# QK-norm of a streaming encoder layer: sums of squares as two-row products, inverse roots spread through memory

## The reference

```
z  = rms_norm(x) @ w_in
qa = rms_norm(qa.reshape(B, T, 8, 64), qn_a)      # FoX queries; the keys ka likewise
qb = rms_norm(qb.reshape(B, T, 4, 2, 64), qn_b)   # Diff queries; the keys kb likewise
rms_norm(x, g) = x * rsqrt(mean(x*x over the last 64) + eps) * g
```

## Time and profile before

| | |
|---|---|
| median of 3 runs | 2223.88 us (2221.85 to 2227.34) |
| profiled execution, span from first to last instruction | 2221.3 us |
| TensorE busy | 2098.9 us, 94% |
| VectorE busy | 963.1 us, 43% |
| ScalarE busy | 792.3 us, 36% |
| GpSimd busy | 109.1 us, 5% |
| mean granted TensorE clock | 0.950 |

### The profile page before, as it was taken

One profiled execution on the slowest core, in us unless ns is written; L12 is line 12 of the kernel. 1 busy time (PEld: TensorE's weight loads), 2 busy tenths in 40 slices (PEclk: granted clock), 3 DMA queues, 4 the chain that ended last, 5 costly groups with the idle time before them and its releaser, 6 DMA issues.

```text
span 2221.3 us, 33304 instructions
## 1 busy us (share of the span) xinstructions
PE 2098.9 (94%) x12679; PEld 1980.5 (89%) x12679; DVE 963.1 (43%) x1613; ACT 792.3 (36%) x1427; POOL 109.1 (5%) x182
## 2 busy tenths in 40 slices
PE   5999999999999999999869999999999999999997
PEld 4988898898988889898758999999999999999987
DVE  5433334324344353444436523755355435544542
ACT  3444444435344454545332223433122212212321
POOL 3100100101001000100000000000000000000001
PEclk8998999889999899989779999999999999999999
DMA  5220401303212130212124322011111111111112
GB/s 195 70 68 10 129 20 30 118 10 97 60 30 79 26 92 9 86 30 58 41 100 128 130 87 68 29 47 43 53 34 46 38 52 38 37 49 46 37 52 72
DMA packets 149045, 135.64 MB, mean 61 GB/s; under 512 B 5160, under 2 KB 131218, under 8 KB 148960
## 3 DMA queue, kind: packets, MB, share of 16 engines
q1 hardware_dynamic: 130368, 68.95, 11.0%
q0 software_dynamic: 18592, 65.46, 9.0%
HBM read 103.56 MB, written 30.83 MB: 61 GB/s over the span
## 4 chain that ended last, share of the span: by engine, by line
PE 84%; DVE 6%; issue 3%; ACT 3%; DMA 2%; POOL 0%; DVEq 0%; ACTq 0%; SPq 0%; POOLq 0%
PE bank L613 44%; PE psS L613 21%; PE psO L613 14%; PE psT L800 3%; DMA gate<-gate_scr 2%; DVE pT_l L1319 1%; ACT pT_h L958 1%; PE bank L673 1%; DVE m_a L1539 1%; PE psT L613 1%; DVE sc L1472 0%; DVE m_b L1539 0%; DVE w_l L1319 0%; PE bank L728 0%; PE psT L642 0%
## 5 line engine op out<-in xcount | busy, mean ns | idle before, releaser
L613 PE MATMUL bank<-xn_hi,w_h 128*128 128x364 f32 (+1 forms) x952 | 336.7, 354 | 22.0 <-DVE xn_lo L1319 11.7
L613 PE MATMUL bank<-xn_lo,w_h 128*128 128x364 f32 (+1 forms) x952 | 325.5, 342 | 0.0
L613 PE MATMUL bank<-xn_hi,w_l 128*128 128x364 f32 (+1 forms) x952 | 324.8, 341 | 0.0
L613 PEld LDWEIGHTS bank<-xn_hi,w_h 128*128 128x128 f32 x952 | 190.8, 200 | 33.3 <-issue 21.0
L958 ACT ACTIVATE w_h<-wraw 128x1024 fp32r<-128x1024 f32 x133 | 139.6, 1050 | 216.4 <-PE psO L613 206.5
L1134 ACT ACTIVATE sc<-sc,small 128x1024 f32<-128x1024 f32 (+5 forms) x144 | 118.7, 824 | 250.1 <-DVE small L1457 250.0
L613 PEld LDWEIGHTS bank<-xn_lo,w_h 128*128 128x128 f32 x952 | 190.7, 200 | 0.0
L613 PEld LDWEIGHTS bank<-xn_hi,w_l 128*128 128x128 f32 x952 | 189.5, 199 | 0.0
L1319 DVE TENSOR_TENSOR w_l<-wraw,w_h 128x1024 fp32r<-128x1024 f32 x133 | 162.2, 1220 | 39.0 <-ACT w_h L958 38.9
L1258 ACT ACTIVATE ct<-u,vecs 128x1090 f32<-128x1090 f32 x44 | 57.2, 1300 | 327.6 <-DVE u L1598 327.6
L613 PE MATMUL psS<-x_l,w_h 128*128 128x364 f32 (+1 forms) x528 | 173.7, 329 | 0.0
(11 more groups left out here) (310 smaller groups left out, 4600.1 us busy)
## 6 DMA issues: line engine op xcount, KB each, us to landing
wraw<-in_w_up SPq DMA_DIRECT2D x44, 512.0 KB, 3.9
wraw<-in_w_in SPq DMA_DIRECT2D x41, 512.0 KB, 4.0
gate<-gate_scr POOLq DMA_DIRECT2D x16, 544.0 KB, 4.4
wraw<-in_w_down SPq DMA_DIRECT2D x16, 384.0 KB, 3.2
wraw<-in_w_down SPq DMA_DIRECT2D x16, 320.0 KB, 2.9
x_scr<-xT POOLq DMA_DIRECT2D x8, 544.0 KB, 3.7
cum_s<-c_scr POOLq DMA_DIRECT2D x8, 544.0 KB, 7.9
gate_scr<-zv POOLq DMA_DIRECT2D x8, 544.0 KB, 5.0
```

The costliest lines, as they stand in the source:

```text
L613: return pe.matmul(out, w, x, start=first, stop=last, **kw)
```

## The change

The sums of squares become products with `half_ones` as the weights (two columns) and the squares as the moving operand, 364 columns at a time. Six jobs SQ0 to SQ2 and SK0 to SK2 take the place of SS0 and SS1; ScalarE copies each [2, 364] result to the first two rows of `sqq` or `sqk`. SP writes these rows to memory (`ms_scr`), reads them back as [128, 34] into `meansq`, and after Sqrt and reciprocal writes `root` out (`rt_scr`) and loads each of the four rows into the 64 partitions of its head. NQ and NK go; a unit has 32 jobs in place of 34. The plans are rearranged around this. In SP's queue the new steps stand between the loads of G0 and G1.

```diff
-        gaps = {-1: [["Q0"], ["Q1"]], 7: [["Q2"], ["SS0", "K0"]], 8: [["K1"], ["K2", "V0"]],
-                6: [["SS1"], ["V1"]], 5: [["V2"], ["NQ0", "VT0"]], 4: [["NQ1", "VT1"], ["VT2", "NQ2"]],
-                3: [["G00"], ["NK0", "NK1"]], 2: [["NK2", "KC0"], ["G01"]], 1: [["KT0", "KT1"], ["G02"]],
-                0: [["KT2", "KC1", "/G10"], ["G10"]]}
+        gaps = {-1: [["Q0"], ["Q1"]], 7: [["Q2"], ["SQ0", "SQ1", "K0"]], 8: [["SQ2", "K1"], ["K2", "V0"]],
+                6: [["SK0", "SK1"], ["SK2", "V1"]], 5: [["V2"], ["VT0"]], 4: [["VT1"], ["VT2"]],
+                3: [["G00"], ["KC0"]], 2: [["KC1"], ["G01"]], 1: [["KT0", "KT1"], ["G02"]],
+                0: [["KT2", "/G10"], ["G10"]]}
...
-        gaps = {-1: [["Q0"], ["Q1"]], 7: [[], ["Q2", "K0"]], 8: [["SS0", "KC0"], ["K1"]],
-                6: [["K2"], ["SS1", "V0"]], 5: [["V1"], ["V2"]], 4: [["VT0", "VT1"], ["VT2", "G00"]],
-                3: [["NQ0", "NQ1"], ["G01", "NQ2"]], 2: [["NK0"], ["G02"]], 1: [["NK1", "NK2"], ["G10"]],
-                0: [["KT0", "KT1"], ["KT2", "KC1"]]}
+        gaps = {-1: [["Q0"], ["Q1"]], 7: [[], ["Q2", "K0"]], 8: [["SQ0", "SQ1", "KC0"], ["SQ2", "K1"]],
+                6: [["K2"], ["SK0", "SK1", "V0"]], 5: [["SK2", "V1"], ["V2"]], 4: [["VT0"], ["VT1", "G00"]],
+                3: [["VT2"], ["G01"]], 2: [["KC1"], ["G02"]], 1: [["KT0"], ["G10"]], 0: [["KT1"], ["KT2"]]}
...
-PROLOGUE_PLAN = ["F0", "F1", "F2", ("W", "K"), "Q0", "Q1", "Q2", ("FORGET",), ("W", "V"), "K0", "K1", "K2",
-                 "KC0", "KC1", "SS0", "SS1", ("NORM",), "V0", "NQ0", "NQ1", "NQ2", "NK0", "NK1", "NK2", ("SCALE",),
-                 "V1", "KT0", "KT1", "KT2", ("SPLIT", 0, 1), "V2", "VT0", "VT1", "VT2", ("WFIRST",), ("SPLIT", 2)]
+PROLOGUE_PLAN = ["F0", "F1", "F2", ("W", "K"), "Q0", "Q1", "Q2", ("FORGET",), ("W", "V"), "K0", "SQ0",
+                 "K1", "SQ1", "K2", "SQ2", "SK0", "SK1", "SK2", "KC0", "KC1", "V0", "V1", ("NORM",), "V2", "VT0", "VT1",
+                 "VT2", ("SCALE",), "KT0", "KT1", "KT2", ("SPLIT", 0, 1), ("WFIRST",), ("SPLIT", 2)]
...
+    if nxt:                                   # Sqrt and reciprocal move from behind SS1 to behind V2
+        then["V2"] = then["V2"] + [("ROOT",)]
+        later["V2"] = later["V2"] + [("RD",)]
+        later[SCALE_AFTER[kind]] = later.get(SCALE_AFTER[kind], []) + [("SCALE",)]
+SCALE_AFTER = {"A": "KC1", "B": "G01"}
...
+        def spread_roots(count, n):
+            sp.wait_ge(S["pj_d"], count)
+            sp.dma_start(ms_scr[0:2], sqq[0:2, :]).then_inc(S["ms_o"], 16)
+            sp.dma_start(ms_scr[2:4], sqk[0:2, :]).then_inc(S["ms_o"], 16)
+            sp.wait_ge(S["ms_o"], n * 32 + 32)
+            sp.dma_start(meansq[:], ms_scr.rearrange("r t -> (r t)").rearrange("(p c) -> p c", p=P)
+                         ).then_inc(S["ms_i"], 16)
+            sp.wait_ge(S["rt_d"], n + 1)
+            sp.dma_start(rt_scr.rearrange("r t -> (r t)").rearrange("(p c) -> p c", p=P), root[:]
+                         ).then_inc(S["rt_o"], 16)
+            sp.wait_ge(S["rt_o"], n * 16 + 16)
+            for x, dst in enumerate((sqq, sqk)):
+                for h in range(2):
+                    sp.dma_start(dst[DH * h:DH * h + DH, :], rt_scr[2 * x + h:2 * x + h + 1].broadcast_to([DH, T])
+                                 ).then_inc(S["rt_i"], 16)
+        spread_roots(J1["SK2"], 0)            # prologue, before the loads of unit 0
...
-            for g in range(2):
-                load_w(wraw[:], U.block(f"G{g}"), gv[U.u][g])
+            load_w(wraw[:], U.block("G0"), gv[U.u][0])
+            if U.nxt:
+                spread_roots(U.j0 + U.job["SK2"], U.u + 1)
+            load_w(wraw[:], U.block("G1"), gv[U.u][1])
...
+            elif kind in ("SQ", "SK"):
+                pe.wait_ge(S["pj_d"], base_of(f"{kind[1]}{c}"))
+                c0, m = CHUNKS[c]
+                sq = sqq if kind == "SQ" else sqk
+                r = mm(bank[0:2, 0:m], half_ones[:, 0:P:DH], sq[:, c0:c0 + m], True, True)
...
-            act.wait_ge(S["pj_d"], J1["SS1"] if U is None else U.j0 + U.job["SS1"])
+            act.wait_ge(S["ms_i"], 16 if U is None else U.u * 16 + 32)
             act.activation(root[:], meansq[:], ACT.Sqrt, bias=eps_t).then_inc(S["sq_rt"], 1)
...
+            dve.wait_ge(S["rt_i"], 64 if U is None else U.u * 64 + 128)
+            for z, q, g in ((zq, sqq, gq_a if kind == "A" else gq_b), (zk, sqk, gk_a if kind == "A" else gk_b)):
                 r = dve.scalar_tensor_tensor(z[:], z[:], g, q[:], ALU.mult, ALU.mult)
```

More of the change, by code:

```diff
@@ L87, in unit_plan @@
     end = ["SPLIT", "G11", "G12", "OT0", "OT1", "OT2"] if nxt else ["OT0", "OT1", "OT2"]
-    then = {"SS1": [("ROOT",)], **({"G02": [("H", "FIRST")]} if nxt else {}),
+    then = {**({"G02": [("H", "FIRST")]} if nxt else {}),
             **{a: [("H", b)] for a, b in WEIGHTS_AFTER[nxt].items()}}
-    later = {"SS1": [("RD",)], "NK2": [("SCALE",)], **({"G02": [("L", "FIRST")]} if nxt else {}),
+    later = {**({"G02": [("L", "FIRST")]} if nxt else {}),
              **{a: [("L", b)] for a, b in WEIGHTS_AFTER[nxt].items()}}
+    if nxt:
+        then["V2"] = then["V2"] + [("ROOT",)]
+        later["V2"] = later["V2"] + [("RD",)]
+        later[SCALE_AFTER[kind]] = later.get(SCALE_AFTER[kind], []) + [("SCALE",)]
     pending = []
@@ L189, in build @@
     c_scr = nc.dram_tensor("c_scr", (2, H_A, T), F32).ap()
+    ms_scr = nc.dram_tensor("ms_scr", (4, T), F32).ap()
+    rt_scr = nc.dram_tensor("rt_scr", (4, T), F32).ap()
     def alloc(stack):
@@ L212, in build @@
     rsub = small[:, 26:35]
-    meansq = sb("meansq", [P, NT, 2, 2])
-    root = sb("root", [P, NT, 2, 2])
+    meansq = sb("meansq", [P, 4 * T // P])
+    root = sb("root", [P, 4 * T // P])
     inv0 = sb("inv0", [P, NT])
@@ L693, in job @@
                     return
[L694 to L697 removed]
+            elif kind in ("SQ", "SK"):
+                pe.wait_ge(S["pj_d"], base_of(f"{kind[1]}{c}"))
+                if U is None and name == "SQ0":
                     pe.wait_ge(S["cst"], 5)
[L699 to L711 removed]
+                c0, m = CHUNKS[c]
+                sq = sqq if kind == "SQ" else sqk
+                r = mm(bank[0:2, 0:m], half_ones[:, 0:P:DH], sq[:, c0:c0 + m], True, True)
             elif kind == "VT":
@@ L1024, in evacuate @@
                 r = copy(zv[:, tok], src)
-            elif kind == "SS":
-                r = copy(meansq[:, 0:8, c, :], bank[:, 0:16].rearrange("p (t h) -> p t h", h=2))
-                r = copy(meansq[0:T_S, 8, c, :], bank[0:T_S, 16:18])
-            elif kind in ("NQ", "NK"):
-                t0, m = TGROUPS[c][0] * P, (3 * P if c < 2 else 2 * P + T_S)
-                r = copy((sqq if kind == "NQ" else sqk)[:, t0:t0 + m], bank[:, 0:m])
+            elif kind in ("SQ", "SK"):
+                c0, m = CHUNKS[c]
+                r = copy((sqq if kind == "SQ" else sqk)[0:2, c0:c0 + m], bank[0:2, 0:m])
             elif kind in ("VT", "KT"):
@@ L1375, in normalize @@
             kind = "A" if U is None else U.next_kind
-            for name, z, q, g in (("NQ2", zq, sqq, gq_a if kind == "A" else gq_b),
-                                  ("NK2", zk, sqk, gk_a if kind == "A" else gk_b)):
-                dve.wait_ge(S["pj_d"], J1[name] if U is None else U.j0 + U.job[name])
+            dve.wait_ge(S["rt_i"], 64 if U is None else U.u * 64 + 128)
+            for z, q, g in ((zq, sqq, gq_a if kind == "A" else gq_b), (zk, sqk, gk_a if kind == "A" else gk_b)):
                 r = dve.scalar_tensor_tensor(z[:], z[:], g, q[:], ALU.mult, ALU.mult)
```

22 lines of the change are left out of this document (1 added, 21 removed).

## The result

| | before | after |
|---|---|---|
| median | 2224.41 us (4 runs, 2221.85 to 2227.34) | 2275.95 us (4 runs, 2263.74 to 2286.26) |
| ratio after to before | | 1.023, 95% interval 1.0195 to 1.0265 |
| span of the profiled execution | 2221.3 us | 2262.2 us |
| mean granted clock | 0.950 | 0.941 |

The profiled execution is the quickest of the four after; the others had mean clocks of 0.937, 0.933 and 0.928 and took 2273.6, 2278.4 and 2286.3 us.

What follows compares the result with a forecast made beforehand. TensorE, busy 94% of the span, was taken to bound the kernel. Work and waits +28.3 and clock -2.4 gave +26 on the profiled 2221.3 us, plus 2.6 to the median: 2250 us, range 2217 to 2277.

Steps and rivals of the forecast that it cites:

- Dearer: Rival: two-row products do not hold the clock and every stall brings a long dip; +15, 2265 us; chance 0.20.
- Work and waits, clock aside: Whole kernel without clock effects: prologue +5.0, four A units -2.4, three B units +25.7, together +28.3 us.
- K1: Prologue: with SQ0 between, K1 waits for K0's evacuation by ScalarE; 4.5 us later, 3.9 idle.
- A's K0: A units, tile 7, second map: K0 waits for SQ0's evacuation behind the exp; 2.4 us later, 3.1 idle.
- KC0: B units, tile 8, first map: KC0 waits for SQ0's copy behind the exp; +2.6 us, 3.3 idle.
- ScalarE before G1's copy: B units: G1's load queues behind roots and spread on SP; ScalarE stalls 5.9 us, +7.2 us a unit (bounds +4 to +10).
- KT0: Prologue: TensorE idles 7.3 us before KT0, waiting for roots, spread and scaling.
- B's tile 4: B units: the root's 1.6 us on ScalarE delays tile 4's product, which already waits 0.72 us for VectorE.
- The trip: Roots through memory in B units: small write 2.3 us, spreading loads of 1.1 MB about 6.4 us.
- Net -2: Clock over the whole kernel: 44 us returned by the sums, 42 lost to new stalls; bounds -24 to +16.
- six stalls: B units: two new stalls in each, priced at 3.5 us of clock apiece, 21 us together.
- the root at tile 5: A units: the moved root delays the copy of the next transposes on ScalarE; next product waits, +0.8 us.

Runs made afterwards that it cites:

- g3: Changed kernel with each two-row product of the sums issued twice, the second overwriting the first with the same values: 2283.06 us, ratio 1.0288.
- e1: Changed kernel with the square-sum jobs spread over the slots, so no long job stands two places behind a short one of its slot: 2246.19 us, ratio 1.0106.
- e2: Changed kernel with G1's load issued before the roots are written out and spread: 2250.21 us, ratio 1.0131.
- f4: Kernel before the change with each square-sum job cut from nine two-column products to one of 18 columns (norm computed wrongly): 2166.73 us, ratio 0.975.
- e0: The repeat: changed kernel as it is, run again as base for the other runs: 2273.58 us, ratio 1.0222.
- f2: Changed kernel with the root and its table loads behind the copy of transposed probabilities of A's tile 5 (second map) and B's tile 4: 2268.2 us, ratio 1.0197.
- f3: Changed kernel with the edits of e1, e2 and f2, B's scaling moved, and the prologue's K1 and root reordered: 2200.82 us, ratio 0.9895.
- g1: f3 with the root and table loads ahead of G0's first chunk on ScalarE, and A's last V transposes in their old place: 2191.22 us, ratio 0.986.
- e3: Changed kernel with the Sqrt of units 0 to 6 replaced by a copy, so no table loads (norm computed wrongly): 2238.19 us, ratio 1.0078.
- f1: Changed kernel with three more products, never read, ahead of the transposes of each V block: 2263.0 us, ratio 1.015.
- g2: f3 with the Sqrt of units 0 to 6 replaced by a copy, so no table loads (norm computed wrongly): 2177.63 us, ratio 0.9797.
- h1: g1 with A's jobs reordered so each conversion ahead of a copy of transposed probabilities has a long product beside it: 2175.96 us, ratio 0.979.

## Why the prediction was right, and which term was off

Forecast 2250, measured 2276: slower, as said, but by 51.5 us and not by 26. The time lies 1 us inside the upper end of the range (2277), so that the range held by little; the rival "Dearer" (2265) came nearer in number, though g3 shows that half of its mechanism is false.

**Work and waits, clock aside: right in sum, and in part by luck.** Up to unit 7's first scores the trace is 46.7 us longer. TensorE idles 66.5 us more than before (125.6 against 59.1), and 41.6 us of work are gone: +24.9, where the sum had +28.3. By stage, idle time added against what the sum implied (its term plus the 5.2 us a norm that left, with the 1.0 us wait before unit 0's Q0 counted in A): prologue 15.7 against 11.2, A 13.1 against 17.4, B 37.7 against 41.3. In A 7.0 us of this are the two waits at the loop's turn that went, of which the prediction used one as a price for the clock and expected neither to go. Without them A's waits are 20.1 and the sum +32. So the new waits were put some 4 us too low, and an unforeseen gain of 7 hid it.

**Step by step.** K1 3.54 us of idle (3.9 said), A's K0 2.93 (3.1), KC0 3.33 (3.3), ScalarE before G1's copy 4.96 (5.9), KT0 8.91 (7.3). The first scores came at 135.5 (131.3): V's transposes end 1.6 us later than said, the wait behind them is 1.6 longer, and from KT0 to the scores it takes 6.5 us and not 5.5, at half clock. The mechanisms are also shown by removal: e1 takes the bank waits away and 27 us, e2 the queue order and 23. In B's tile 4 the delay of the root was put at 1.6 us on ScalarE; the wait went from 0.72 to 2.67.

**Durations.** Two-row products: 0.32 us said, 0.31 to 0.35 from start to start. The trip was quicker in the write of the roots (1.5 to 1.8 us against 2.3) and slower in the spread (in unit 5 first issue 920.9, last landing 928.4, 7.5 us against 6.4; up to 8.1 in the others); these nearly cancel. The Trainium skill (DMA: Bandwidth & Descriptors, section "Anatomy of one DMA - SWDGE (gpsimd) path") gives 2.0 us fixed plus bytes over 436 GB/s. The trace differs on both sides: 1.5 to 1.8 us for 17 KB, 7.5 for the 1.1 MB that it puts at 4.6; these DMAs leave SP's queue, though, not GpSimd's.

**The clock: the term that was off.** It is "Net -2": 44 us given back by the sums, 42 lost to new stalls. TensorE's busy time up to unit 6 fell by 19.9 us (1000.2 to 980.3) where 41.6 of work left: the clock took 22, not -2. By stage: prologue 0, A +6, B +16. The first half of the step had the mechanism right and the size a little high: by f4 the two-column sums cost 32 or 33 us of clock, not 44, and by g3 two-row products cost none, against the rival "Dearer". The second half was too low in two places.

In B, six stalls were priced at 21 us, and more places than these lose the clock. The half clock of the first trace after (81.9 us, against 34.2 before) stands in four places: 27.4 us at KC0's bank wait (units 5 and 6), 13.6 behind the root at tile 4, 30.6 at the wait for G1's weights, 10.2 behind a wait of 1.4 us for VectorE's scores, which has no term. e1 has none of it at KC0, e2 6.8 at G1; other stretches grow in their place, so that the totals fall by less.

In A, the step priced K0's stall (2.0; the trace has 3.4 to 6.8 us of half clock behind it in three units, none in unit 3) and gave the root at tile 5 0.8 us of waiting and no clock. But this 1.32 us stands where the spreading products went and only thin ones are left. The traces count it. With a wait of 1.3 to 1.6 us at tiles 5 to 3 (after, e0, e1, e2, f2, f3, g1, g3), a stretch of 10 to 20 us at half clock begins in or behind it in 25 of 32 A units, and the four units together have 68 to 94 us. Without it (e3, f1, g2, h1) no stretch that begins in any of 16 A units is over 6.8 us, though all four kernels have a wait of 1.3 us later, at tile 2. So all that the sums gave back in A was lost again: 75.1 us of half clock before, 75.9 after.

The rest, from 41 us in the traces to 51.5 at the median, is the same term. The repeat's trace is 13.8 us longer than the first, with 31 us more half clock and no more idle time: A's stretch in three units and not in two, and two stretches of 10.2 us in B, behind waits of 0.6 us, that the first trace does not have. The eight runs of the changed kernel lie within 22.5 us; the kernel before, in 34 runs, within 15.

Open is why the same wait starts the long stretch in one unit and not in the next, and why the two waits at the loop's turn went.

## What to carry to other kernels

Removing thin work from the engine that bounds also removes what covered the others' small jobs: look, for each filler that goes, at which conversion, table load or weight split stood beside it. A trip through memory is cheap when nothing that is needed soon is queued behind it; put urgent loads first, and judge a queue by what follows. Put each side job of an engine (root, weight split) in a slot with a long product, and price a wait in a thin stretch by the clock behind it, not by its length.

## What the runs showed of the hardware

- Half clock can follow a short wait: 1.3 to 1.6 us of idle between thin products, and 10 to 20.5 us at 1.2 GHz in or behind it in 25 of 32 A units (13.7 to 17.1 in all four of g1). The same wait did not always do it (units 1 and 2 after), and two executions of one kernel differ by 13.8 us with 31 us more at half clock (after, e0).
- Products that move two columns for each load of 128 weight columns pulled the clock down, in the units without any wait of TensorE beside them: f4, with 16 of 18 instructions left out of two jobs in eight norms, is 57.6 us faster, over half of it clock. Products with two weight columns that stream 364 did not.
- The table loads of ScalarE are 1.28 us each here, two of them and the root 2.9 us; to leave them out is worth 35 us in the changed kernel (e3), by what they delayed; h1, which has them in other places, is no slower than g2, which has not.
